# Delta net: the inverse's first levels on diagonal 32x32 blocks, the last one as a 32x32 block beside the diagonal

## The reference

```python
kb = k * beta[..., None]
a_strict = jnp.einsum('bhnid,bhnjd->bhnij', kb, k) * decay * (idx[:, None] > idx[None, :])
rhs = jnp.concatenate([v * beta[..., None], kb * jnp.exp(gc)[..., None]], axis=-1)
sol = lax.linalg.triangular_solve(a_strict + jnp.eye(C), rhs, left_side=True, lower=True, unit_diagonal=True)
u, w = sol[..., :dv], sol[..., dv:]
```

## Time and profile before

| | |
|---|---|
| profiled execution | 2932.93 us |
| its span | 2930.9 us, 46270 instructions |
| mean granted TensorE clock | 0.958 |
| TensorE matmuls busy | 2728.1 us, 93% |
| TensorE weight loads busy | 1829.9 us, 62% |
| VectorE / ScalarE / GpSimd busy | 1048.0 / 644.9 / 520.1 us |
| delta net, first to last head's inverse | 1406.22 to 2071 us of the span |

### The profile page before, as it was taken

The page is one execution under the profiler, slowest core; times in us unless marked ns, Lnnn a source line. Parts: engine busy times, 40 slices in busy tenths (PEclk is TensorE's granted clock), DMA queues, the critical chain, the costliest instruction groups (busy, mean ns, idle before and its releaser), DMA issues. The chain is left out here.

```text
span 2930.9 us, 46270 instructions
## 1 busy us (share of the span) xinstructions
PE 2728.1 (93%) x18862; PEld 1829.9 (62%) x18863; DVE 1048.0 (36%) x2314; ACT 644.9 (22%) x1362; POOL 520.1 (18%) x466
## 2 busy tenths in 40 slices
PE   6699999796999999987999999999886999999997
PEld 6355555453555555554776677766635887688774
DVE  5244544416776664012444344443402110010100
ACT  0344544302222220004223232232102111010000
POOL 0111111003332224211333122331100010000000
PEclk6899999898999999998999999999887999999999
DMA  6142241202333333100111101110018997495731
GB/s 222 45 121 63 63 126 42 89 1 86 102 113 114 114 117 82 49 11 22 31 31 31 30 2 31 31 30 9 7 52 301 348 321 221 159 296 163 251 108 29
DMA packets 309234, 297.73 MB, mean 102 GB/s; under 512 B 5712, under 2 KB 268880, under 8 KB 308944
## 3 DMA queue, kind: packets, MB, share of 16 engines
q1 hardware_dynamic: 303024, 273.30, 30.4%
q0 software_dynamic: 4896, 17.83, 2.3%
q10 hardware_dynamic: 1152, 4.19, 0.4%
HBM read 281.14 MB, written 12.58 MB: 100 GB/s over the span
## 5 line engine op out<-in xcount | busy, mean ns | idle before, releaser
L1601 PE MATMUL bank<-work,weight_ring 128*128 128x128 f32 (+1 forms) x2048 | 315.4, 317 | 6.1 <-ACT work L1651 6.1
L2014 PE MATMUL bank<-hidden,weight_ring 128*128 128x512 f32 (+1 forms) x768 | 310.2, 538 | 1.8 <-ACT work L2336 1.8
L1601 PEld LDWEIGHTS bank<-work,weight_ring 128*128 128x128 f32 x2048 | 291.8, 193 | 27.7 <-issue 8.1
L601 PE MATMUL bank<-weight_ring,hidden 128*128 128x384 f32 x760 | 266.5, 495 | 4.9 <-ACT work L730 4.6
L1147 PE MATMUL bank<-hidden,weight_ring 128*128 128x384 f32 x704 | 238.2, 492 | 18.4 <-issue 18.4
L1268 DVE SCALAR_TENSOR_TENSOR weight_ring<-weight_ring,silu_c 128x256 f32<-128x256 f32 x308 | 217.8, 748 | 5.5
L601 PEld LDWEIGHTS bank<-weight_ring,hidden 128*128 128x128 f32 x760 | 137.9, 191 | 109.0 <-ACT work L730 16.6
L1147 PEld LDWEIGHTS bank<-hidden,weight_ring 128*128 128x128 f32 x704 | 133.1, 192 | 107.2 <-issue 20.6
L2014 PEld LDWEIGHTS bank<-hidden,weight_ring 128*128 128x128 f32 x768 | 135.5, 190 | 82.8 <-issue 68.7
L1147 PE MATMUL bank<-weight_ring 128*128 128x384 f32 x528 | 182.4, 496 | 0.3 <-DVE work L1276 0.3
L1756 DVE TENSOR_TENSOR work<-work,bank 128x128 f32<-128x128 f32 (+1 forms) x88 | 29.7, 337 | 426.0 <-ACT work L1656 426.0
(11 more groups left out here) (330 smaller groups left out, 3775.5 us busy)
## 6 DMA issues: line engine op xcount, KB each, us to landing
weight_ring<-in_moe_w_in SPq DMA_DIRECT2D x64, 1024.0 KB, 10.4
weight_ring<-in_ada_w SPq DMA_DIRECT2D x38, 1024.0 KB, 5.2
weight_ring<-in_ffn_w_in SPq DMA_DIRECT2D x44, 512.0 KB, 4.9
hidden<-in_moe_w_out SPq DMA_DIRECT2D x8, 2816.0 KB, 10.5
residual<-in_moe_w_out SPq DMA_DIRECT2D x8, 2816.0 KB, 16.1
work<-in_moe_w_in SPq DMA_DIRECT2D x16, 1024.0 KB, 8.8
weight_ring<-in_na_w_qkv SPq DMA_DIRECT2D x24, 512.0 KB, 7.7
weight_ring<-in_gdn_w_qkv SPq DMA_DIRECT2D x24, 512.0 KB, 5.4
```

The source lines that it names most:

```text
L601: mm = nc.tensor.matmul(m.psum[6][:, 0:3 * P], m.H[:, k, t * P:(t + 1) * P], weights(u)[:, k, :], start=(k == 0), stop=(k == KD - 1))
L1601: mm = nc.tensor.matmul(B[c % 4][:, ab * HALF:ab * HALF + N], w[:, ab, k, (c % 2) * P:(c % 2 + 1) * P], XG[:, k, 0:N], start=(k == 0), sto ...
L2014: mm = nc.tensor.matmul(B[b][:, c0:c0 + t1 - t0], W[:, s, k, :], m.H[:, k, t0:t1], start=(k == 0), stop=(k == KD - 1))
```

## The change

Levels 0 to 4 join blocks up to 32x32, so they stay inside the two 32x32 blocks on the diagonal of each chunk. These now lie alone, as `[128 partitions, 12, 32]` (TD, UD, AM, Y), four blocks above each other on partitions 0, 32, 64 and 96, and the function diagonal multiplies them with 24 calls of 32x32 and 32 streamed columns, one of the four row positions after the other, each into the same rows of PSUM. ScalarE, VectorE and GpSimd handle 192 columns where they had 384. The turn of the whole matrices (turn_whole) uses 24 calls with 32 output rows each and swaps the halves of 32 in the odd ones, so that the block beside the diagonal lies on the rows that the last level reads. The last level (function last_level) computes only the block beside the diagonal: 12 calls for y and 12 for u on the two row positions that matter for a direction, with A itself instead of a masked copy, so the masks of level 5 go. At level 4 VectorE writes U in four operations on 32 partitions each, at level 5 in two. U is cleared once before the first head; the zero blocks stay zero. In the kernel after, HALF_ROWS, wt, cu and the scan are as before.

```diff
+    r32, c32 = row % CQ, col[:, 0:CQ]
+    for n in range(5):
         s = 1 << n
-        pair = (r64 // (2 * s) == c64 // (2 * s)) & (r64 // s != c64 // s)
-        c[:, C_LEVF + n * CH:C_LEVF + (n + 1) * CH] = pair & (r64 > c64)
-        c[:, C_LEVB + n * CH:C_LEVB + (n + 1) * CH] = pair & (r64 < c64)
+        pair = (r32 // (2 * s) == c32 // (2 * s)) & (r32 // s != c32 // s)
+        c[:, C_LEVF + n * CQ:C_LEVF + (n + 1) * CQ] = pair & (r32 > c32)
+        c[:, C_LEVB + n * CQ:C_LEVB + (n + 1) * CQ] = pair & (r32 < c32)
+    c[:, C_TURN64:C_TURN64 + CH] = r64 == (c64 + CQ) % CH
+    c[:, C_ID32:C_ID32 + CQ] = r32 == c32
...
-    A, T, U, AM, Y = (tiles(PROBLEMS, CH) for _ in range(5))
+
+
+    A, T, U = (tiles(PROBLEMS, CH) for _ in range(3))
+    TD, UD, AM, Y = (tiles(PROBLEMS, CQ) for _ in range(4))
...
+    ident64 = (const(m, C_ID64, CH), const(m, C_TURN64, CH))
+    ident32 = const(m, C_ID32, CQ)
...
+    ROWS32 = [slice(CQ * r, CQ * r + CQ) for r in range(4)]
...
+    def quarters(b):
+        return B[b][:, 0:TILES * CQ].rearrange("p (n t) -> p n t", n=TILES)
...
-                def turn(b, X, d, name):
+                def turn_whole(b, d, name):
                     for n in range(TILES):
-                        for c in HALF_ROWS:
-                            mm = nc.tensor.matmul(blocks(b, TILES)[c, n, :], X[c, TILES * d + n, :], ident64[c, :], start=True, stop=True)
+                        for r, rows in enumerate(ROWS32):
+                            c = HALF_ROWS[r // 2]
+                            mm = nc.tensor.matmul(blocks(b, TILES)[rows, n, :], T[c, TILES * d + n, CQ * (r % 2):CQ * (r % 2) + CQ],
+                                                  ident64[r % 2][c, :], start=True, stop=True)
+                    mm.then_inc(pe_step, TE.step(name))
+
+                def diagonal(b, X, Z, name):
+                    for n in range(TILES):
+                        for r in ROWS32:
+                            mm = nc.tensor.matmul(quarters(b)[r, n, :], X[r, n, :], Z[r, :] if len(Z.shape) == 2 else Z[r, n, :],
+                                                  start=True, stop=True)
                     mm.then_inc(pe_step, TE.step(name))
...
-                turn(0, T, 0, "at0")
+                turn_whole(0, 0, "at0")
                 pe.wait_ge(dve_step, VE.after(h, "ad1"))
-                turn(1, T, 1, "at1")
+                turn_whole(1, 1, "at1")
...
-                    turn(d, T, d, f"tt{d}")
+                    diagonal(d, TD[:, of(d), :], ident32, f"tt{d}")
...
                             pe.wait_ge(dve_step, VE.after(h, f"U{l - 1}.{d}"))
-                        for n in range(TILES):
-                            for c in HALF_ROWS:
-                                mm = nc.tensor.matmul(blocks(2 * d, TILES)[c, n, :], AM[c, TILES * d + n, :], U[c, TILES * d + n, :],
-                                                      start=True, stop=True)
-                        mm.then_inc(pe_step, TE.step(f"y{l}.{d}"))
+                        diagonal(2 * d, AM[:, of(d), :], UD[:, of(d), :], f"y{l}.{d}")
                         if l == 1:
                             ws(11) if d == 0 else kv(11)
                     for d in range(2):
                         if l > 1:
                             pe.wait_ge(dve_step, VE.after(h, f"T{l - 1}.{d}"))
                         pe.wait_ge(act_step, SC.after(h, f"Y{l}.{d}"))
-                        for n in range(TILES):
-                            for c in HALF_ROWS:
-                                mm = nc.tensor.matmul(blocks(2 * d, TILES)[c, n, :], T[c, TILES * d + n, :], Y[c, TILES * d + n, :],
-                                                      start=True, stop=True)
-                        mm.then_inc(pe_step, TE.step(f"u{l}.{d}"))
+                        diagonal(2 * d, TD[:, of(d), :], Y[:, of(d), :], f"u{l}.{d}")
                         if l == 1 and d == 1 and scan:
                             pe.wait_ge(act_scan_step, SS.before(h, "gate"))
-                        if l < LEVELS - 1:
-                            for n in range(TILES):
-                                for c in HALF_ROWS:
-                                    mm = nc.tensor.matmul(blocks(2 * d + 1, TILES)[c, n, :], Y[c, TILES * d + n, :], T[c, TILES * d + n, :],
-                                                          start=True, stop=True)
-                            mm.then_inc(pe_step, TE.step(f"t{l}.{d}"))
-
-                for l in range(1, LEVELS):
+                        diagonal(2 * d + 1, Y[:, of(d), :], TD[:, of(d), :], f"t{l}.{d}")
+
+                def last_level():
+
+                    l = LEVELS - 1
+                    for d in range(2):
+                        pe.wait_ge(dve_step, VE.after(h, f"U{l - 1}.{d}"))
+                        for n in range(TILES):
+                            for r in (1 - d, 3 - d):
+                                own = slice(CQ * (r % 2), CQ * (r % 2) + CQ)
+                                mm = nc.tensor.matmul(quarters(2 * d)[ROWS32[r ^ 1], n, :], A[ROWS32[r], TILES * d + n, CQ:CH],
+                                                      U[ROWS32[r], TILES * d + n, own], start=True, stop=True)
+                        mm.then_inc(pe_step, TE.step(f"y{l}.{d}"))
+                    for d in range(2):
+                        pe.wait_ge(dve_step, VE.after(h, f"T{l - 1}.{d}"))
+                        pe.wait_ge(act_step, SC.after(h, f"Y{l}.{d}"))
+                        for n in range(TILES):
+                            for r in (d, 2 + d):
+                                mm = nc.tensor.matmul(quarters(2 * d)[ROWS32[r], n, :], TD[ROWS32[r], TILES * d + n, :],
+                                                      Y[ROWS32[r], TILES * d + n, :], start=True, stop=True)
+                        mm.then_inc(pe_step, TE.step(f"u{l}.{d}"))
+
+                for l in range(1, LEVELS - 1):
                     level(l)
                     if l == 2:
                         norm_sums()
+                last_level()
...
-                    nc.scalar.copy(U[:, of(d), :], blocks(d, TILES)).then_inc(act_step, SC.step(f"U{d}"))
+                    nc.scalar.copy(UD[:, of(d), :], quarters(d)).then_inc(act_step, SC.step(f"U{d}"))
...
-                        nc.scalar.copy(Y[:, of(d), :], blocks(2 * d, TILES)).then_inc(act_step, SC.step(f"Y{l}.{d}"))
+                        nc.scalar.copy(Y[:, of(d), :], quarters(2 * d)).then_inc(act_step, SC.step(f"Y{l}.{d}"))
...
-                    nc.gpsimd.tensor_tensor(AM[:, of(d), :], A[:, of(d), :], same(const(m, lev[d] + l * CH, CH), TILES), ALU.mult)\
+                    nc.gpsimd.tensor_tensor(AM[:, of(d), :], A[:, of(d), 0:CQ], same(const(m, lev[d] + l * CQ, CQ), TILES, CQ), ALU.mult)\
...
-                for d in range(2):
-                    level_mask(5, d)
...
+            nc.vector.memset(U, 0.0).then_inc(pre_dve, 1)
...
-                    nc.vector.tensor_tensor(T[:, of(d), :], same(ident64, TILES), AM[:, of(d), :], ALU.subtract)\
+                    nc.vector.tensor_tensor(TD[:, of(d), :], same(ident32, TILES, CQ), AM[:, of(d), :], ALU.subtract)\
...
-                        nc.vector.tensor_tensor(U[:, of(d), :], U[:, of(d), :], blocks(2 * d, TILES), ALU.subtract)\
-                            .then_inc(dve_step, VE.step(f"U{l}.{d}"))
+                        if l < LEVELS - 2:
+                            op = nc.vector.tensor_tensor(UD[:, of(d), :], UD[:, of(d), :], quarters(2 * d), ALU.subtract)
+                        elif l == LEVELS - 2:
+                            for r, rows in enumerate(ROWS32):
+                                own = slice(CQ * (r % 2), CQ * (r % 2) + CQ)
+                                op = nc.vector.tensor_tensor(U[rows, of(d), own], UD[rows, of(d), :], quarters(2 * d)[rows], ALU.subtract)
+                        else:
+                            for r in (d, 2 + d):
+                                other = slice(CQ * (1 - d), CQ * (1 - d) + CQ)
+                                op = nc.vector.tensor_scalar(U[ROWS32[r], of(d), other], quarters(2 * d)[ROWS32[r]], -1.0, None, ALU.mult)
+                        op.then_inc(dve_step, VE.step(f"U{l}.{d}"))
                         if l < LEVELS - 1:
                             dve.wait_ge(pe_step, TE.after(h, f"t{l}.{d}"))
-                            nc.vector.tensor_tensor(T[:, of(d), :], T[:, of(d), :], blocks(2 * d + 1, TILES), ALU.subtract)\
+                            nc.vector.tensor_tensor(TD[:, of(d), :], TD[:, of(d), :], quarters(2 * d + 1), ALU.subtract)\
```

More of the change, by code:

```diff
@@ L54 @@
 CH = 64
+CQ = 32
 C_IDENT = 0
@@ L66 @@
 C_LEVF = C_BEFORE + P
-C_LEVB = C_LEVF + 6 * CH
-C_CUM64F = C_LEVB + 6 * CH
+C_LEVB = C_LEVF + 5 * CQ
+C_CUM64F = C_LEVB + 5 * CQ
 C_CUM64B = C_CUM64F + CH
@@ L72 @@
 C_ID64 = C_STRICTB + CH
-C_IOTA = C_ID64 + CH
+C_TURN64 = C_ID64 + CH
+C_ID32 = C_TURN64 + CH
+C_IOTA = C_ID32 + CQ
 C_SLOT = C_IOTA + EXPERTS
@@ L100, in constants @@
     r64, c64 = row % CH, col[:, 0:CH]
```

(20 more changed lines are left out.)

## The result

The change made the kernel slower: 3073.93 us (median of 4 runs, 3073.51 to 3080.51) against 2930.59 us (4 runs, 2927.93 to 2940.53), a ratio of 1.0488 with a 95% interval of 1.046 to 1.0516. The profiled execution has a span of 3071.6 us.

A forecast was written before the change was run, and what follows sets the result against it. TensorE's order of work was taken as the bound. Savings of 0.62 + 1.86 + 1.70 + 1.70 + 1.5 = 7.4 us a head, 59 for eight, less 0.5 for clearing U, gave 2872 us after a 2.4 us median correction; range 2855 to 3020.

The forecast's parts named there:

- What bounds the kernel: Whole kernel: TensorE, busy 93% of the span, sets the end of the inverse; what shortens its work comes off the total.
- Time of a diagonal product: Inverse: a product of 24 calls in four 32x32 tiles takes 0.39 us instead of 0.70.
- the supply falls short a little: Rival, TensorE's instruction fetch: 1.24 us a packet, a level takes 3 to 4.3 us; 2890 to 2920 us, chance 0.15.
- back to back they just suffice: Instruction packets in levels 2 to 4: one needed every 1.2 us, each taking 1.24 us, enough if without gaps.
- Records come no faster than now: Rival, TensorE's products: the sequencer's pace limits them; at 29.2 ns a pair +148 us, 3079 us; chance 0.27.
- The clock falls: Rival, TensorE's granted clock: small tiles and 0.31 us waits lower it, products 0.78 us; 2935 to 2950 us, chance 0.05.
- Turns, levels, level 5: Per head: turns save 0.62 us (at unchanged), level 1 1.86, levels 2 and 3 1.70 each, levels 4 and 5 1.5.
- The wait for ScalarE of 0.3 us: Levels 2 to 4: TensorE waits 0.31 us for ScalarE's copy ahead of u.0, which the 0.70 us products nearly covered.
- U4's four operations: Level 4: VectorE writes U in steps of 0.30 us, four in 1.20; at 0.55 each, 16 us of gain are lost.
- Sum: All savings together: 7.4 us a head, 59 us for eight heads, less 0.5 for clearing U.

The follow-up runs named there:

- loop32: Kernel after with TensorE's levels 1 to 4 as a hardware loop of four passes, and some scan, norm and value work moved: 2993.4 us, ratio 1.0203 to before.
- loop64: Kernel before, 64x64 tiles kept, with levels 1 to 4 in a hardware loop and the same moves as loop32: 2972.3 us, ratio 1.0144 to before.
- lastblock: Kernel before with only the last level changed to 32x32 blocks off the diagonal, without its masks: 2928.4 us, ratio 0.9995 to before.
- reorder32: Kernel after with the moves of loop32 alone, levels 1 to 4 still in straight code without the loop: 3082.7 us, one run.

## Why the prediction was wrong

*What bounds the kernel.* Right: TensorE's order of work sets the end of a head, and what came on top of each head came on top of the total.

*Time of a diagonal product.* The step that failed: a product every 0.39 us, with the supply of instructions at no cost. The tiles were nearly right. Where instructions are at hand, one product takes 0.55 to 0.56 us up to a matmul of another shape and two take 0.98 (loop32, 1524.68 and 1525.39; after, 1507.13), so a product is 0.43 us and the change of shape 0.13; the four tiles do run at once. The supply was what failed: 24 products of levels 1 to 4 were to take 9.4 us, and their instructions alone are nine packets. What gave 3073.9 is the term of the rival "the supply falls short a little": it took 1.24 us for a packet, which is how long the transfer lasts. What counts is the time from one packet to the next when TensorE uses them up, 3.95 us, and "back to back they just suffice" was wrong by a factor of about three. 2304 instructions of levels 1 to 4 are nine packets, 35.5 us; where levels 1 to 4 took 20.1 before (1496.76 to 1516.87): +15 us a head, had the rival been worked out with it. The earlier trace rows held a warning, though not the number: six packets in 31 us are one every 5 us, and 256 instructions of 64x64 products go in 3.74 us, so that before was already near the pace of supply, without a hole.

*Records come no faster than now.* That the time came near its upper value (3079) is luck: the records are not slow, they are missing. The Trainium skill, "TensorE: Matmul & The Clock Gate", section "Wait — 56ns, not 53.3ns?", has a floor of 25 ns from start to start; the trace doesn't agree for four tiles, 96 matmul records in 0.98 us are 10.2 ns each.

*The clock falls.* Priced as a case of its own at 5 in 100, and it came as the companion of the holes: 4.0 us in wt and cu of head 1, and at half clock 0.79 us for one product up to another shape and 1.43 for two (loop32), where full clock has 0.56 and 0.98. loop32 against loop64 shows it without the long holes: 0.86 against 0.97. That small tiles alone bring it down isn't isolated, since loop32 keeps one hole of 1.85 us a head.

*Turns, levels, level 5.* at stayed at 0.7 a product (96 records in 1.47 us, before 48 in 1.54). The wait for ScalarE of 0.3 us in each level did not show, for supply came later. U4's four operations took 0.35 us each, 0.30 was taken. Level 5 by itself gained 1.4 us in head 1 of lastblock, as the forecast's 1.5 for levels 4 and 5.

*Sum.* 7.4 us a head less were forecast, 18.5 more came. Of the 25.9 between them 15.5 are idle time, nearly all of it for instructions, and 4.0 wt and cu (both read in head 1). The rest, 6.4, is what is left over; products and norm rows at half clock and products of 0.43 instead of 0.39 are the likely cause, not added up.

## What to carry to other kernels

Before an operation is cut into more, smaller ones, count the instructions (an fp32 matmul call is four here) and hold them against the pace at which straight code is supplied, 256 in some 4 us on TensorE in this kernel: an engine that stands at "issue" every 128 pairs has met it. A loop or long matmuls between the short ones took the holes away here, fewer instructions a call made them fewer; but look at the granted clock too: it fell in every run with 32x32 products in levels 1 to 4, least with the long fillers between them (0.96 in the mean), and the full-size work behind them pays.

## What the runs showed of the hardware

- Straight code: 256 TensorE instructions (16 KB) in 3.5 to 4.3 us in after (3.95 in head 1), 3.3 to 4.3 in reorder32; the packet itself takes 1.0 to 1.2 us in the mean (1.6% of 16 engines over 40 us for ten, and the earlier trace rows), and the next one begins only 1.0 to 1.9 us after TensorE has started on it. In loop32's passes of 576 instructions no hole came after the first pass. The Trainium skill, "Advanced Engine Details and Errata", section "ISA Cache", has a line of 16 KB or 256 instructions, with which the holes agree, and a cache of 32 KB, 128 KB on TensorE; a pass of 36 KB in loop32 ran without a hole, which agrees with the 128 KB and not with the "Only 2 cache lines!" that the section has beside it.
- Four 32x32 tiles take 96 fp32 matmul records in 0.98 us at full clock (loop32, 1525.39), 1.43 at half clock (1515.01): 1.5 times as long, where wt goes from 2.8 to 5.3 us.
- A change of tile shape behind a product takes 0.13 us after 32x32 tiles (loop32) and 0.15 after 64x64 tiles (before, loop64). A product of 64x64 tiles takes 0.70 us in straight code and in a loop.
